# Routing on raw rows with the ranks ahead of the gates, and a gate sum moved into a joint, in a two-block transformer kernel on one Trainium2 core

## The reference

```python
h = h + spatial_gating(u, vv, c_w_s[j], c_b_s[j]) @ c_w_out[j]
h = h + moe_swiglu(rms_norm(h, ln_ffn[i]), router_w[j], moe_w1[j], moe_w3[j], moe_w2[j])

def moe_swiglu(h, router_w, w1, w3, w2):          # top 2 of 8 experts
    logits = jnp.einsum('nd,de->ne', xt, router_w, preferred_element_type=jnp.float32)
    top_val, top_idx = lax.top_k(logits, TOP_K)
    gates = jax.nn.softmax(top_val, axis=-1)
    ...                                           # tokens sorted by expert, each expert on its own rows
    contrib = y_sorted * gate_flat[order][:, None].astype(h.dtype)
```

```python
mod = c_act @ w_ada[l] + b_ada[l]
sh1, sc1, g1, sh2, sc2, g2 = [t[:, None, :] for t in jnp.split(mod, N_ADA, axis=-1)]
h = rmsnorm(x, norm_mix_g[l]) * (1.0 + sc1) + sh1
...
x = x + g1 * (o @ w_out[l])
h = rmsnorm(x, norm_mlp_g[l]) * (1.0 + sc2) + sh2
x = x + g2 * (jnp.square(jax.nn.relu(h @ w_up[l])) @ w_down[l])
```

## Time and profile before

| | |
|---|---|
| time before, median of 3 runs | 1949.4 us (1948.94 to 1952.83) |
| the profiled execution's own time | 1949.06 us |
| its span, first to last instruction | 1947.3 us |
| mean granted TensorE clock | 0.988 |
| PE busy | 1871.4 us, 96% of the span |
| DVE, ACT, POOL busy | 79%, 61%, 3% |
| HBM | 271 GB/s over the span |
| chain of work that ended last | PE 89%, DVE 5%, ACT 3% |

### The profile page before, as it was taken

How to read it: one execution, slowest core, us unless ns; L and a number is a source line. 1 busy time by engine, 2 the same in 40 slices (tenths; PEclk the granted TensorE clock), 3 DMA queues, 4 the chain that set the end, 5 groups by cost and what they waited for, 6 DMA issues and landing times.

```text
span 1947.3 us, 27157 instructions
## 1 busy us (share of the span) xinstructions
PE 1871.4 (96%) x10640; PEld 1618.8 (83%) x10640; DVE 1534.0 (79%) x2105; ACT 1195.7 (61%) x1642; POOL 50.4 (3%) x56
## 2 busy tenths in 40 slices
PE   7999999999999999999999999899899989999998
PEld 7889998777888888888888887698789978878997
DVE  5768887567999999999999998657589985756565
ACT  4444445635888888888888887557554446744443
POOL 0010000002000000000000010000000000000000
PEclk9999999999999999999999999999999999999999
DMA  7348886744999999999999999343278974324551
GB/s 313 130 158 307 327 345 256 283 170 151 423 387 382 388 372 387 379 384 376 387 376 386 368 407 376 120 152 111 85 262 337 356 269 149 114 82 178 181 194 44
DMA packets 75902, 528.39 MB, mean 271 GB/s; under 512 B 8659, under 2 KB 9043, under 8 KB 14323
## 3 DMA queue, kind: packets, MB, share of 16 engines
q1 hardware_dynamic: 69536, 504.40, 67.8%
q10 hardware_dynamic: 3060, 11.02, 1.6%
q0 software_dynamic: 3168, 11.14, 1.4%
HBM read 515.90 MB, written 11.01 MB: 271 GB/s over the span
## 4 chain that ended last, share of the span: by engine, by line
PE 89%; DVE 5%; ACT 3%; issue 1%; POOL 1%; DMA 0%; POOLq 0%; SPq 0%; ACTq 0%; DVEq 0%
PE ps L554 28%; PE ps L556 27%; PE ps L555 27%; PE ps L775 2%; DVE w_lo L1396 1%; PE ps L727 1%; ACT w_hi L2301 1%; PE ps L990 1%; PE ps L740 1%; POOL stat L2812 1%; DMA ring<-in_stream 0%; ACT xT L2311 0%; PE ps L818 0%; ACT score L2422 0%; PE ps L973 0%
## 5 line engine op out<-in xcount | busy, mean ns | idle before, releaser
L2301 ACT ACTIVATE w_hi<-ring 128x1024 fp32r<-128x1024 f32 x862 | 911.2, 1061 | 592.9 <-PE ps L556 587.5
L1396 DVE TENSOR_TENSOR w_lo<-ring,w_hi 128x1024 fp32r<-128x1024 f32 x862 | 1040.4, 1222 | 254.3 <-ACT w_hi L2301 242.9
L554 PE MATMUL ps<-w_hi,x_hi 128*128 128x512 f32 (+1 forms) x1056 | 410.8, 391 | 8.7 <-DVE w_lo L1396 3.6
L556 PE MATMUL ps<-w_hi,x_lo 128*128 128x512 f32 (+1 forms) x1056 | 400.2, 381 | 0.0
L555 PE MATMUL ps<-w_lo,x_hi 128*128 128x512 f32 (+1 forms) x1056 | 399.2, 380 | 0.0
L554 PE MATMUL ps<-x_hi,w_hi 128*128 128x256 f32 x1248 | 359.7, 288 | 5.7 <-DVE x_lo L1511 4.6
L555 PE MATMUL ps<-x_lo,w_hi 128*128 128x256 f32 x1248 | 355.1, 285 | 0.0
L556 PE MATMUL ps<-x_hi,w_lo 128*128 128x256 f32 x1248 | 354.9, 284 | 0.0
L554 PE MATMUL ps<-w_hi,h_hi 128*128 128x512 f32 x732 | 285.1, 390 | 0.9 <-DVE h_lo L2028 0.9
L555 PE MATMUL ps<-w_lo,h_hi 128*128 128x512 f32 x732 | 284.9, 389 | 0.0
L556 PE MATMUL ps<-w_hi,h_lo 128*128 128x512 f32 x732 | 284.3, 388 | 0.0
(11 more groups left out here) (298 smaller groups left out, 1306.8 us busy)
## 6 DMA issues: line engine op xcount, KB each, us to landing
ring<-in_stream SPq DMA_DIRECT2D x479, 1024.0 KB, 6.9
x_store<-arena ACTq DMA_DIRECT2D x1, 4096.0 KB, 28.9
arena<-x_store POOLq DMA_DIRECT2D x7, 512.0 KB, 8.4
y_store<-y_slots POOLq DMA_DIRECT2D x7, 512.0 KB, 8.7
con<-in_consts ACTq DMA_DIRECT2D x1, 2048.0 KB, 21.5
arena<-in_ln_rows ACTq DMA_DIRECT2D x3, 512.0 KB, 4.3
resid<-in_x SPq DMA_DIRECT2D x1, 1024.0 KB, 6.3
arena<-in_c ACTq DMA_DIRECT2D x2, 512.0 KB, 3.8
```

The lines of the kernel that those rows point to most:

```text
L554: pe.matmul(out_, lhs[0], rhs[0], start=start, stop=False)
L556: return pe.matmul(out_, lhs[1], rhs[0], start=False, stop=stop)
L1396: dve.tensor_tensor(lo, ring[:, q % RING, a:a + HALF], hi.bitcast(F32), ALU.subtract)\
L2301: act.activation(half_buffer(m)[0], ring[:, q % RING, a:a + HALF], ACT.Copy).then_inc(hi_ready, 1)
```

## The change

In the router head the raw rows of `resid` are transposed, each half tile as soon as its sum is written, and copied by ACT into `xT`; the gain is multiplied into the router's weights beforehand. The logits of each tile have their own bank and semaphore. DVE marks the chosen experts per tile and asks for the ranks; the rows are scaled on DVE beside that, `place` and `sel` come next, and the gates, with the exponential now scaled by the row's inverse root, and `most_i` follow behind `sel` (`weigh`). The `keep_warm` of 18, 4 and 18 become 4 and 4. ACT's order changes: the squares of tile 0 go ahead of the first half of the expert stage, and the copies of the transposes ahead of the squares of tile 1 and of the two halves behind them.

In the second model the gate sums of layer 1 move ahead of `rowsT(8)`, and their copies on ACT between the squares and the modulation.

```diff
                     else:
                         pe.wait_ge(rows_scaled, SCALED_AT[k] + n)
 
-                if k in (1, 4, 6, 7, 9):
+                if k in (1, 6, 7, 9):
                     keep_warm(18, 6 if k in (7, 9) else 2)
                 scaled(1)
...
@@ -935,22 +936,29 @@
                 row_tile(c0 + k, (x_hi[:, k, :], x_lo[:, k, :]), 4, False, False)
             last_rows(c0 + 5, [(x_hi[:, k, :], x_lo[:, k, :]) for k in range(5, KT)], 4, False)
 
-            rowsT(4)
-            keep_warm(4, 2)
-            pe.wait_ge(gained, GAINED_AT[4] + 4)
+            for t in range(QB):
+                for half in range(2):
+                    pe.wait_ge(resid_ready, 4 * 3 + (2, 3 + half)[t])
+                    for i in range(4):
+                        f = 4 * half + i
+                        last = pe.transpose(ps[:, 2 * t + half, i * P:(i + 1) * P], resid[:, t, f * P:(f + 1) * P], ident)
+                    last.then_inc(rowsT_ready, 1)
             for t in range(QB):
                 for k in range(KT):
-                    last = pe.matmul(ps[:, 0, t * 8:(t + 1) * 8], xT[:, k, t * P:(t + 1) * P],
+                    if k % 4 == 0:
+                        pe.wait_ge(router_rows, 2 * t + k // 4 + 1)
+                    last = pe.matmul(ps[:, 4 + 3 * t, 0:8], xT[:, k, t * P:(t + 1) * P],
                                      col("router", k * 8, 8), start=k == 0, stop=k == KT - 1)
-            last.then_inc(logits_ready, 1)
-
-            keep_warm(18, 2)
+                last.then_inc(logits_ready, 1)
+
+            keep_warm(4, 2)
             pe.wait_ge(member_ready, 1)
-            pe.matmul(ps[:, 1, 0:8], col("before"), member[:, 0, :], start=True, stop=True)
-            pe.matmul(ps[:, 1, 8:16], col("before"), member[:, 1, :], start=True, stop=False)
-            pe.matmul(ps[:, 1, 8:16], ones[:, :], member[:, 0, :], start=False, stop=True)
+            pe.matmul(ps[:, 5, 0:8], col("before"), member[:, 0, :], start=True, stop=True)
+            pe.wait_ge(member_ready, 2)
+            pe.matmul(ps[:, 5, 8:16], col("before"), member[:, 1, :], start=True, stop=False)
+            pe.matmul(ps[:, 5, 8:16], ones[:, :], member[:, 0, :], start=False, stop=True).then_inc(ranks_ready, 1)
             for t in range(QB):
-                last = pe.matmul(ps[:, 1, 16:24], ones[:, :], member[:, t, :], start=t == 0, stop=t == 1)
+                last = pe.matmul(ps[:, 3, 0:8], ones[:, :], member[:, t, :], start=t == 0, stop=t == 1)
             last.then_inc(ranks_ready, 1)
 
             def gather(w, ready):
...
@@ -1138,7 +1147,10 @@
                     pe.wait_ge(ple_gated, 8)
                     rowsT(6)
                 else:
+                    pe.wait_ge(folded, 4 * ADA_SLOTS)
+                    ada_gates((2, 3, 0, 1))
                     rowsT(8)
+                    pe.wait_ge(gates_kept, 8)
                 job0 = 10 + IN_SLOTS * l
 
                 def in_tile(t, halves=(0, 1)):
@@ -1150,12 +1162,7 @@
 
                 in_tile(0)
                 in_tile(1)
-                if l == 1:
-                    pe.wait_ge(folded, 4 * ADA_SLOTS)
-                    ada_gates((4, 5, 6, 7))
                 in_tile(2)
-                if l == 1:
-                    pe.wait_ge(gates_kept, 8)
                 value_rows(n0 + B_V)
 
                 pe.wait_ge(squares_ready, l + 1)
...
@@ -1936,48 +1936,49 @@
                 keep_gated(t)
                 if t == 0:
                     split_to(reach(u0 + 7))
+            link(dve.tensor_tensor(col("router").rearrange("p (k e) -> p k e", e=NE),
+                                   col("router").rearrange("p (k e) -> p k e", e=NE), bc(gain(4), NE), ALU.mult))
             add_branch(4, W_COUT + 4, first_half=1)
...
+            ask_root(4, 0)
+            scale(4, 0)
             for t in range(QB):
+                dve.wait_ge(logits_ready, t + 1)
+                link(dve.tensor_copy(logit[:, t, :], ps[:, 4 + 3 * t, 0:8]))
                 link(dve.max(top[:, t, :], logit[:, t, :]))
                 link(dve.max_index(topi[:, t, :], top[:, t, :], logit[:, t, :]))
                 link(dve.tensor_copy(route[:, t, 0, :], topi[:, t, :]))
...
+                for n in range(2):
+                    ins = dve.tensor_scalar(chosen[:, t, n, :], col("iota"), route[:, t, 0, n:n + 1], None, ALU.is_equal)
+                link(ins)
+                dve.tensor_tensor(member[:, t, :], chosen[:, t, 0, :], chosen[:, t, 1, :], ALU.add).then_inc(member_ready, 1)
+                dve.tensor_tensor(route[:, t, 1, 0:1], top[:, t, 1:2], top[:, t, 0:1], ALU.subtract)                    .then_inc(route_asked, 1)
                 if t == 0:
...
+                    ask_root(4, 1)
+            dve.wait_ge(member_ready, 2)
+            dve.tensor_scalar(apart[:, :, :], member[:, :, :], -1000.0, 1000.0, ALU.mult, ALU.add)
+            dve.memset(gate[:, :, NE:NE + 1], 0.0)
+            link(dve.memset(place[:, :, NE:NE + 1], -1.0))
+            scale(4, 1)
             dve.wait_ge(ranks_ready, 1)
...
+            link(dve.tensor_tensor(place[:, :, 0:NE], ps[:, 5, 0:16].rearrange("p (b e) -> p b e", b=QB), apart[:, :, :],
+                                   ALU.add))
+
+            def weigh():
+
+                dve.wait_ge(route_exp, 2)
+                prob = [route[:, :, 1, n:n + 1].rearrange("p b o -> p (b o)") for n in range(5)]
+                link(dve.tensor_scalar(prob[2], prob[1], 1.0, None, ALU.add))
+                link(dve.reciprocal(prob[3], prob[2]))
+                link(dve.tensor_tensor(prob[4], prob[1], prob[3], ALU.mult))
+                for t in range(QB):
+                    for n in range(2):
+                        ins = dve.tensor_scalar(route[:, t, 2 + n, :], chosen[:, t, n, :], route[:, t, 1, 3 + n:4 + n],
+                                                None, ALU.mult)
+                link(ins)
...
@@ -2114,6 +2115,7 @@
                 dve.wait_ge(w.merged, e(1, 2))
 
             select(moe, 0)
+            weigh()
             take(moe, [1, 2])
             for s in range(STEPS):
                 moe_step(s)
@@ -2531,6 +2533,8 @@
 
                 for n in range(4):
                     act.wait_ge(gates_summed, 4 * l + n + 1)
+                    if (l, n) == (1, 2):
+                        act.wait_ge(resid_ready, 4 * 8)
                     act.activation(grow[:, n // 2, n % 2 * BANK:(n % 2 + 1) * BANK], ps[:, banks[n], :], ACT.Copy)\
                         .then_inc(gates_kept, 1)
 
@@ -2576,11 +2580,24 @@
             act.wait_ge(vn_ready, 2)
             act.dma_start(moe_gain, ln_rows[2].partition_broadcast(P)).then_inc(moe_gain_in, 16)
             keep_gated(1)
+            split_to(2 * (W_COUT + 4))
+            act.wait_ge(resid_ready, 4 * 3 + 2)
+            square(resid[:, 0, :], v_rows.rearrange("p b n -> p (b n)")[:, 0:D], 8)
             split_to(2 * (W_COUT + 4) + 1)
-            square_rows(4, 2 * (W_COUT + 4) + PAIRS)
-            act.wait_ge(route_asked, 1)
             for t in range(QB):
-                act.activation(route[:, t, 1, 1:2], route[:, t, 1, 0:1], ACT.Exp).then_inc(route_exp, 1)
+                for half in range(2):
+                    act.wait_ge(rowsT_ready, 4 * 4 + 2 * t + half + 1)
+                    act.activation(xT[:, 4 * half:4 * half + 4, t * P:(t + 1) * P],
+                                   ps[:, 2 * t + half, :].rearrange("p (f s) -> p f s", f=4), ACT.Copy)\
+                        .then_inc(router_rows, 1)
+            for half in range(2):
+                square(resid[:, 1, half * BANK:(half + 1) * BANK], v_rows.rearrange("p b n -> p (b n)")[:, D + half * BANK:D + (half + 1) * BANK], 9 + half)
+            split_to(2 * (W_COUT + 4) + PAIRS)
+            act.wait_ge(root_ready, 12)
+            for t in range(QB):
+                act.wait_ge(route_asked, t + 1)
+                act.activation(route[:, t, 1, 1:2], route[:, t, 1, 0:1], ACT.Exp, scale=stat[:, t:t + 1])\
+                    .then_inc(route_exp, 1)
 
             def take(w, counts, c0=0):
                 for h in range(2):
@@ -2701,12 +2718,11 @@
             for l in range(2):
                 n0 = W_BLK + l * B_ALL
                 split_to(2 * (n0 + B_IN) + 1)
-                norm_hi(6 + 2 * l, 2 * (n0 + B_IN) + PAIRS)
+                norm_hi(6 + 2 * l, 2 * (n0 + B_IN) + PAIRS,
+                        (lambda: keep_gates(1, (2, 3, 0, 1))) if l == 1 else None)
                 h0 = 2 * n0
                 keep_input(n0, 0)
                 keep_input(n0, 1)
-                if l == 1:
-                    keep_gates(1, (4, 5, 6, 7))
                 keep_input(n0, 2)
                 slots_done(n0 + B_V + 2)
                 act.activation(v2.rearrange("p b n -> p (b n)"), bank(4, 2), ACT.Copy).then_inc(vrows_kept, 1)
```

55 lines of the change are left out of this document (10 added, 45 removed).

## The result

| | before | changed |
|---|---|---|
| median of four executions, side by side | 1949.17 us (1948.72 to 1952.83) | 1937.83 us (1936.39 to 1940.42) |
| ratio | | 0.9944, 95% interval 0.9932 to 0.9955 |
| second comparison, five executions against eleven | 1948.63 us | 1938.08 us, ratio 0.9944 (0.9931 to 0.9957) |
| profiled execution, its span | 1949.06, 1947.3 us | 1940.42, 1938.7 us |
| mean granted clock of it | 0.988 | 0.987 |

The change is faster by 0.56%, and the median is the predicted 1937.8. The terms behind it are not all as predicted. The profiled execution happens to be the slowest of the four.

The account below looks back on a forecast made before the run. PE, busy 96% of the span, was taken as the bound, so gains lie where it waits or does unneeded work. Head 9.5 less clock 1.3 (8.2) plus gate sums 3.4 is 11.6 off, forecast 1937.8 us, range 1935.0 to 1942.0.

Parts of the forecast that it names:

- Gate sums, 3.4: Block layer 1: moving the sums into PE's wait in the joint ahead of it gains 3.4 us.
- each cover: Joint: sums fill PE's 3.37 us idle, ACT's copies (2.4) fit its 3.48 idle; DVE idled 1.65 before its half.
- Head at the upper clock, 9.5: Router head: the gather starts at 449.7 instead of 459.2, 9.5 us gained if the clock stays at 2.4 GHz.
- The late start: Start of the router head: ACT's squares go first, so tile 1's additions end 0.7 us later, a loss on the path.
- rival C: Router head: `weigh` isn't covered, a late exponential pushes `x_lo`; 1939.6, or 1941 with 1.5 us delay; chance 0.08.
- Clock, 1.3: Router head: the clock falls during or just behind the logits and costs 1.3 us, within bounds 0 and 6.2.
- rival B: Router head: clock low for logits, `keep_warm` and most of the gather, costing 5 of the 6.2; 1941.5; chance 0.15.
- the prediction's own signs: Wrong if the gather starts less than 7 us earlier against the branch's end; head clock well below 0.85 means B.
- the 11.6 of the sum: Whole program: net router head 8.2 plus gate sums 3.4 gives 11.6 us off the profiled 1949.06.

Follow-up runs that it names:

- second comparison: The changed kernel run once more on another chip, five rounds beside the kernel before: 1938.08 us, ratio 0.9944.
- first profile: Profiled execution of the changed kernel in its first comparison, the slowest of four: 1940.42 us, router head 20.90 us.
- 8, 0: Changed kernel with eight `keep_warm` behind the logits and none ahead of the gather, instead of four and four: 1938.72 us, ratio 0.9948 to the kernel before.
- gates moved: Kernel before with only the gate sums of block layer 1 moved into the joint: 1945.74 us, ratio 0.9987.
- gates ahead: Changed kernel with `weigh` ahead of the selection matrix instead of behind it, `keep_warm` 4, 4: 1936.60 us, ratio 0.9943 to the kernel before.

## Why the prediction was right

**Gate sums, 3.4: right** in the size and in each cover, and partly for another reason. Layer 1 is 3.3 to 3.7 us shorter (331.9 and 332.0 against 328.6 and 328.3), and the joint is unchanged. The clock was taken at 0. In fact the low stretch moved out of the joint onto the layer's first products and took 1.0 to 1.1 back there (1.3 in the first profile), and a shorter one at the next joint gave 1.3 to 1.4. That these two nearly cancel was not foreseen.

**Head at the upper clock, 9.5: right step by step.** The late start shows: DVE's additions of tile 1 begin 0.94 behind the start of the branch's last product, where it was 0.42 before, so 0.5 later (forecast 0.7). Tile 0's logits are copied 4.83 and 4.67 behind, as the 4.8 of the sum. Tile 1's, at the upper clock, were forecast 6.7 behind and came at 6.45 where the clock was up. From there to `sel` 3.25 against a forecast of 3.4. `weigh` was covered: the table load that rival C feared was over when the first exponential ran at 445.38, the second had ended by 447.5, `weigh` began at 449.28, and DVE idled 4.44 before `x_lo`. Much of that idle time is the slow gather: with the gather at the upper clock, in the run "8, 0", 1.16 were left. So `weigh` was covered there too, with a smaller margin. No profile has the whole head of the changed kernel at the upper clock. Its parts measured at it or bound by DVE, 6.45 to the copy, 3.25 to `sel`, 0.54 to the gather and 5.25 to the first product, add up to 15.5 us against the 15.8 that 25.33 - 9.5 gives.

**Clock, 1.3: wrong, and the term to correct.** The fall was put in the right place, in the logits. Its cost was sized by one stretch as long as that of before. It was 10.2 and 13.7 us long, because after the logits come ranks, waits and a handful of `keep_warm`, which did not end it; the gather ended it. The head was 19.3 and 20.9 instead of the 17.1 that 25.33 - 8.2 gives, so the clock cost 3.5 and 5.1 against those 15.8. That is rival B (5 of 6.2) for the first profile and between it and the forecast for the second. By the prediction's own signs this part failed. It was to be wrong if the gather started less than 7 us earlier against the branch: it started 20.08 us behind the branch's last product before and 13.75 and 13.40 now, 6.3 and 6.7 earlier. And a clock of the head well below 0.85 was to be B: it was 0.67 in the first profile and 0.73 in the second (439.1 to 458.2). I gave B 0.15; the low stretch was 10.2 us or longer in seven of the nine profiles with the changed kernel's logits. B's total of 1941.5 didn't come, for the reasons of the next paragraph. The sentence on which the 1.3 hung was that low stretches end when work returns. In eight of the nine the stretch ended only within the gather, with none, four or eight `keep_warm` ahead of it; I did not ask how much work there was ahead of it.

**Why the total still came out.** Side by side the change gained 11.3 us in the first comparison and 10.6 in the second, against the 11.6 of the sum, and the kernel before took 1949.17, 1948.63 and, in the other two comparisons, 1948.10 and 1947.91, against the 1949.4 on which the forecast stands. So base and gain are both somewhat high, and that cancels. But the two stages by which the sum accounts gained only 7.0 and 9.7 us in the profiles. In the first profile another 1.7 came from the stretch ahead of the head, in the second 1.1 from the MLP of layer 0, both with unchanged code. And the head term isn't off by the whole 2.2 to 3.8 that the two profiles show, because the head of before isn't always 25.33. With the same code it was 26.96 in the profile with the gates moved, where the clock fell a second time, in the gather (window of that kernel):

```profile
461.50:464.90 3.40, 3.40 (x20) 3.40 (x19) 0.69 (x1) 0.60 (x1) 0.00 (x0) 0.54 0.02 5
```

With a head of 25.3 to 27.0 before and 19.3 to 20.9 after, it gained between 4.4 and 7.7. With the 3.4 of the gates the middle is 9.5, and 1 to 2 us of the measured gain remain; they lie in what the clock does elsewhere, and no run here places them. So the direction, the two places and the sizes at the upper clock were earned; that the median came out to the tenth was luck.

## What to carry to other kernels

When steps are taken out between two dense stretches of TensorE, the products kept for the clock go with them. Price the new chain once at each clock level, and look at where the next dense work stands: here the longer stretch decided. Tile 1's logits took 1.8 us at the upper level and 3.4 at the lower. The logits with 128 streamed columns kept the clock up while they ran, in three of three profiles, but their detour cost 1.35 us, so the head was shorter only in the two kernels that also had products in PE's waits. Put such products only where the engine waits at either clock level: at the lower one four of them took 2.05 us instead of 1.18 and became the path. And follow a low stretch that a change has moved: out of the joint it went into the layer behind.

## What the runs showed of the hardware

- The low stretch of the changed kernel (441.7 to 455.3) outlasted four `keep_warm` at 445.45 and four at 449.29, and ended in the gather. In the run with eight behind the logits it was 6.8 us long and over before the gather (3.84).
- Tile 1's logits (16 in the trace's count) took 3.4 us at the lower clock, between the two copies of the changed kernel at 442.22 and 445.63, and 1.8 at the upper one (4.67 to 6.45 behind the branch in the kernel with the gates ahead). So thin products follow the clock. The Trainium skill's rule in "TensorE: Matmul & The Clock Gate", section "LDWEIGHTS (loading the stationary operand)", which names no clock level, would have left them at 1.8; the trace disagrees, as the prediction took it.
- The mean clock of one execution goes with its time: 0.986 with 1949.3 to 1949.5 us and 0.990 with 1943.6 to 1944.9 us for the same kernel. Differences of a us or two between medians of five such executions can't be read as the edit's.
- A tile's logits with 8 loaded and 128 streamed columns are as many products as with 128 loaded and 8 streamed (8, or 16 in the trace's count) and take about as long: 24 span 2.79 us, against 3.74 for 32, so 1.9 a tile. The granted clock was 1.00 while they ran. With the thin ones it fell during them in eight of the nine profiles, and 1.2 us behind them in the ninth, with the gates ahead.
- The table load ahead of the exponential took 1.28 us (444.08), and the exponential started 0.02 behind its end.
